# Norm weights applied to transposed blocks as they leave PSUM, and a shared rotary part copied by GpSimd

## The reference

```python
def _rms(x, g):
    y = xf * lax.rsqrt(jnp.mean(xf * xf, axis=-1, keepdims=True) + EPS)
    return (y * g).astype(x.dtype)
...
cq = (_rms(cq, w["c_cq_g"]) @ w["c_wuq"]).reshape(B, S, C_HEADS, C_QK)
cq = _rms(jnp.concatenate([cq[..., :C_NOPE], _rope(cq[..., C_NOPE:], pos)], axis=-1), w["c_qn_g"])
ckv = _rms(ckv, w["c_ckv_g"])
cpe = _rope(cpe[:, :, None, :], pos)[:, :, 0]
kv = (ckv @ w["c_wukv"]).reshape(B, nk, C_HEADS, C_NOPE + C_V)
ck = jnp.concatenate([kv[..., :C_NOPE], jnp.broadcast_to(cpe[:, :, None, :], (B, nk, C_HEADS, C_ROPE))], axis=-1)
ck = _rms(ck, w["c_kn_g"])
oc = _full_attend(cq[:, :, :, None], ck, kv[..., C_NOPE:], C_QK ** -0.5, q_start, prompt)

mq = _rms(mq.reshape(B, S, M_HEADS, HEAD_DIM), w["m_qn_g"])[:, :, :, None]
om = _attend(mq, mem_k, mem_v, None, HEAD_DIM ** -0.5)
```

## Time and profile before

| | us |
|---|---|
| median of 3 runs | 3257.39 (3252.74 to 3262.34) |
| the profiled execution | 3255.39 |
| its span, first to last instruction | 3253.6 |
| TensorE busy | 2920.4 (90%) |
| VectorE busy | 1807.6 (56%) |
| ScalarE busy | 1197.6 (37%) |
| GpSimd busy | 136.5 (4%) |
| mean granted TensorE clock | 0.936 |

### The profile page before, as it was taken

The page is one execution under the profiler, slowest core; times in us unless marked ns, Lnnn a source line. Parts: engine busy times, 40 slices in busy tenths (PEclk is TensorE's granted clock), DMA queues, the critical chain, the costliest instruction groups (busy, mean ns, idle before and its releaser), DMA issues. The chain is left out here.

```text
span 3253.6 us, 49067 instructions
## 1 busy us (share of the span) xinstructions
PE 2920.4 (90%) x19080; PEld 2750.4 (85%) x19080; DVE 1807.6 (56%) x2899; ACT 1197.6 (37%) x2503; POOL 136.5 (4%) x228
## 2 busy tenths in 40 slices
PE   5888879789899999999968888788789999999997
PEld 3787768579899999999957868667789999999997
DVE  5466765643555555554665586465436555545554
ACT  5556644652322222222246474456413222212222
POOL 0200012000000000000002000120000000000000
PEclk7996989799999999999979979898899999999999
DMA  4110001022111111111031100110411111111111
GB/s 177 32 57 30 23 29 39 8 86 82 52 46 46 41 50 40 46 45 48 20 124 47 48 22 21 40 29 11 150 28 51 47 45 46 43 50 46 40 46 61
DMA packets 182436, 162.11 MB, mean 50 GB/s; under 512 B 14648, under 2 KB 170040, under 8 KB 181688
## 3 DMA queue, kind: packets, MB, share of 16 engines
q1 hardware_dynamic: 182200, 158.81, 15.5%
HBM read 129.92 MB, written 29.06 MB: 49 GB/s over the span
## 5 line engine op out<-in xcount | busy, mean ns | idle before, releaser
L1752 PE MATMUL ps<-h_hi,w_hi 128*128 128x352 f32 x2496 | 550.5, 329 | 49.6 <-DVE w_lo L1863 23.1
L1752 PE MATMUL ps<-h_hi,w_lo 128*128 128x352 f32 x2496 | 544.6, 325 | 6.9 <-issue 6.9
L1752 PE MATMUL ps<-h_lo,w_hi 128*128 128x352 f32 x2496 | 543.1, 326 | 0.0
L1752 PEld LDWEIGHTS ps<-h_hi,w_hi 128*128 128x128 f32 x2496 | 430.3, 192 | 64.7 <-issue 42.2
L1752 PEld LDWEIGHTS ps<-h_hi,w_lo 128*128 128x128 f32 x2496 | 433.3, 190 | 0.0
L1752 PEld LDWEIGHTS ps<-h_lo,w_hi 128*128 128x128 f32 x2496 | 429.7, 190 | 0.0
L2203 ACT ACTIVATE cv<-up,cols 128x1058 f32<-128x1058 f32 x88 | 112.0, 1273 | 737.9 <-issue 697.8
L774 PE MATMUL ps<-w_hi,h_hi 128*128 128x256 f32 (+1 forms) x1152 | 334.5, 290 | 24.1 <-DVE w_lo L944 18.2
L775 PE MATMUL ps<-w_lo,h_hi 128*128 128x256 f32 (+1 forms) x1152 | 328.8, 285 | 0.0
L776 PE MATMUL ps<-w_hi,h_lo 128*128 128x256 f32 (+1 forms) x1152 | 326.6, 284 | 0.0
L2314 DVE TENSOR_TENSOR x_t<-ps,x_t 128x1056 f32<-128x1056 f32 x176 | 221.0, 1256 | 159.5 <-PE ps L1752 158.8
(11 more groups left out here) (211 smaller groups left out, 4275.7 us busy)
## 6 DMA issues: line engine op xcount, KB each, us to landing
stage<-in_f_win SPq DMA_DIRECT2D x88, 512.0 KB, 3.8
stage<-in_f_wout SPq DMA_DIRECT2D x44, 512.0 KB, 3.7
stage<-in_w_in SPq DMA_DIRECT2D x40, 256.0 KB, 4.4
x_spill<-x_t SPq DMA_DIRECT2D x2, 4224.0 KB, 14.3
x_t<-x_spill SPq DMA_DIRECT2D x2, 4224.0 KB
stage<-in_w_o SPq DMA_DIRECT2D x16, 512.0 KB, 4.5
w_raw<-in_w_in SPq DMA_DIRECT2D x24, 256.0 KB, 3.9
o_in<-o_spill SPq DMA_DIRECT2D x8, 528.0 KB, 7.1
```

The lines of the kernel that those rows point to most:

```text
L1752: last = pe.matmul(ps[:, s0 + b, 0:BAND], lh, rh_[:, b * BAND:(b + 1) * BAND], start=(first_k and n == 0), stop=(last_k and n == 2))
```

## The change

For three kinds of pieces (C's queries, C's keys, M's queries; `late_gain`) VectorE writes `res = zs * ri` at once and leaves the norm weight out. After the transposition the head's columns lie on partitions, so the weight is one number per partition: ScalarE multiplies by it in its copy of the high part, and VectorE in the low part, `lo = turned * gain - hi`. The weight tile has one column; it is loaded by DMAs with 4 bytes per partition, for M two of them, since a turned block holds two heads. ScalarE waits once per piece for it.

For C's keys (`shared`) GpSimd copies the rotary part into the four heads of `zs`. It waits for the result two steps back and for the producer of the part; ScalarE's squares wait for it. ScalarE's two remaining copies change places: `zs` first, then v.

```diff
 def first_gains(sp):
     for p in normed:
-        sp.dma_start(p.gain_t[:, :], p.gain.partition_broadcast(P)).then_inc(S.small_loaded, 16)
+        if p.late_gain:
+            for i in range(p.bw // p.hd):
+                sp.dma_start(p.gain_t[i * p.hd:(i + 1) * p.hd, :], p.gain.rearrange("(h o) -> h o", o=1)
+                             ).then_inc(S.small_loaded, 16)
+        else:
+            sp.dma_start(p.gain_t[:, :], p.gain.partition_broadcast(P)).then_inc(S.small_loaded, 16)
...
                     if p.after:
                         src, hi, _ = after_views(g)
-                        act.copy(hi, src).then_inc(S.tr_copied, 1)
+                        if p.late_gain:
+                            if s == 0:
+                                act.wait_ge(S.small_loaded, n_small)
+                                if n_scaled[id(p)]:
+                                    act.wait_ge(S.gain_scaled, n_scaled[id(p)])
+                            act.mul(hi, src, p.gain_t[0:p.bw, 0:1]).then_inc(S.tr_copied, 1)
+                        else:
+                            act.copy(hi, src).then_inc(S.tr_copied, 1)
...
+                if p.late_gain:
+                    dve.tensor_tensor(res[0:r, n % 2, 0:nt * n_el].rearrange("p (t h d) -> p t h d", t=nt, d=hd),
+                                      zv[:, :, 0:n_el].rearrange("p t (h d) -> p t h d", d=hd),
+                                      ri[0:r, 0:gh].rearrange("p (t h) -> p t h", t=nt).unsqueeze(3).broadcast_to([r, nt, H, hd]),
+                                      ALU.mult).then_inc(S.res_done, 1)
+                    return
...
-                dve.tensor_tensor(lo, src, hi.bitcast(F32), ALU.subtract).then_inc(S.tr_low, 1)
+                if p.late_gain:
+                    dve.scalar_tensor_tensor(lo, src, p.gain_t[0:p.bw, 0:1], hi.bitcast(F32), ALU.mult, ALU.subtract
+                                             ).then_inc(S.tr_low, 1)
...
+                if p.shared is not None:
+                    src, from_load, producer = p.shared(s)
+                    pool.wait_ge(S.res_done, n_i[g] - 1)
+                    if from_load:
+                        pool.wait_ge(S.data_loaded0, 16 * len(late_loads))
+                    else:
+                        q, qs = producer
+                        pool.wait_ge(S.res_done, n_i[at[id(q), qs]] + 1)
+                    zp = zs[0:r, n_i[g] % 2, 0:p.n_el].rearrange("p (h c) -> p h c", c=p.hd)
+                    pool.tensor_copy(zp[:, :, 64:96], src.unsqueeze(1).broadcast_to([r, 4, 32])).then_inc(S.pre_rotated, 1)
+                    continue
...
             def copies(t0, nt, r, bank, zs):
-                return [(v_big[0:r, v_tile(t0), :].rearrange("p (h c) -> p h c", c=64), b4[:, :, 64:128]),
-                        (z4[:, :, 64:96], cpe_of(t0, r).unsqueeze(1).broadcast_to([r, 4, 32])),
-                        (z4[:, :, 0:64], b4[:, :, 0:64])]
+                return [(z4[:, :, 0:64], b4[:, :, 0:64]),
+                        (v_big[0:r, v_tile(t0), :].rearrange("p (h c) -> p h c", c=64), b4[:, :, 64:128])]
```

More of the change, by code:

```diff
@@ L581, in pieces_stage @@
         for p in normed:
-            p.gain_t = (gains or w).take("gain", [P, p.hd])
+            p.gain_t = (gains or w).take("gain", [P, 1 if p.late_gain else p.hd])
         G = order or [(p, s) for p in pieces for s in range(len(p.steps))]
@@ L623, in pieces_stage @@
                     split_after[last_of[id(holders[i - 1])]] = p
-        n_small = 16 * len(normed)
+        n_small = 16 * sum(p.bw // p.hd if p.late_gain else 1 for p in normed)
         n_loads = 16 * len(loads)
+        n_scaled, scaled = {}, 0
+        for p in normed:
+            scaled += 1 if p.scale is not None else 0
+            n_scaled[id(p)] = scaled
         res_sem = (S.res_out0, S.res_out1)
@@ L1063, in gpsimd @@
                     norm.pool_low(pool)
-                steps = [g for g in range(NG) if G[g][0].rope_first]
+                steps = [g for g in range(NG) if G[g][0].rope_first or G[g][0].shared is not None]
+                turned_steps = 0
                 for i, g in enumerate(steps):
@@ L1706, in pieces_c, with keys @@
         lat = piece([(t, 1, P) for t in range(4)], raw=lambda s: lat_in[:, s, :], stack="raw", to=lambda t: (ckv_s, None, t * P))
[L1708 removed]
+        def keys(steps, latents, shared, v_tile, placed, to):
             def product(pe, t, r, out):
```

29 lines of the change are left out of this document (19 added, 10 removed).

## The result

| | before | after |
|---|---|---|
| median, same chip | 3257.63 (9 runs, 3249.49 to 3285.07) | 3240.98 (9 runs, 3230.68 to 3244.83) |
| ratio of the runs, 95% interval | | 0.993 (0.9904 to 0.9957) |
| profiled execution / span | 3255.39 / 3253.6 | 3230.68 / 3228.9 |
| mean granted clock in it | 0.936 | 0.940 |

The change gains 0.7% by the ratio of the runs (0.4 to 1.0%, 14 to 31 us), and 17 us between the two medians. The forecast was 12.4 us (3245.0, range 3239 to 3256; a ratio of 0.996). The sign was right, and the gain was larger than predicted. Medians in this document are over all runs of a kernel; ratios and intervals leave out slow ones, those over 1.5% above the fastest of the same kernel.

A forecast was written before the change was run, and what follows sets the result against it. VectorE was taken to pace the key tiles, TensorE nearly the queries. Per layer 2.95 (prompt keys) + 1.97 (cached keys) + 1.04 (C's queries) + 0.25 (M's queries) = 6.21, twice 12.4 us: 3245.0 us, range 3239 to 3256.

The forecast's parts named there:

- The bound and the loop: C's key tiles: VectorE paces at 2.33 us; afterwards the chain through ScalarE and VectorE paces at 2.01 us.
- Rival 1: Key tiles: VectorE and GpSimd block each other, loop 2.41 us, time 3254 on the median; chance 0.12.
- first failed step: C's queries: TensorE's wait for the latent's rotated part limits the gain to 0.26 four times, 1.04 us per layer.
- the first root's 0.42: First prompt key: its root comes 0.42 us earlier, as the last query tile ahead loses its gain step.
- Prompt to cached keys: Last prompt key's root to first cached key's: 0.49 us less per layer, from 0.29 and 0.20.
- M's queries: TensorE paces all but the last step; its last turn's wait for a result shrinks by 0.25 us per layer.
- Rival 2: Key tiles: ScalarE's longer copy and the GpSimd semaphore wait are not hidden, loop 2.15 us, time 3248; chance 0.23.
- The slack of 0.13 and 0.06: Key loop: the room in which ScalarE's longer copy and the extra wait on GpSimd's semaphore were to hide.
- second failed step: Clock at attention C's start: no term in the sum; layer 1 beginning like layer 2, 5 us better (3240), called inside the forecast.
- Rival 3: C's queries at half clock for 22 us per layer: 11 us lost in each, net 9.8 slower, 3267; chance 0.05.

The follow-up runs named there:

- keys_gain: Kernel before plus late gain for C's keys alone, ScalarE still copying the rotary part in the old order; 3266.62 us, ratio 1.002, key loop 2.20.
- keys_shared: Kernel before plus GpSimd's shared copy alone for C's keys, the gain still a VectorE step; 3253.89 us, ratio 0.9993, key loop 2.33.
- pool_eight: Changed kernel with GpSimd's shared copy made eight times in a row, each waiting for the one ahead; 3300.18 us in one execution, loop 3.15.
- only_queries: Kernel before plus late gain for C's queries alone, keys and M's queries as before; 3278.45 us, ratio 1.0092.
- psum_filler: Changed kernel plus a VectorE step as long as the gain step for each C query, one input in PSUM, result unused; 3281.73 us in one execution.
- queries_warm: Kernel with late gain on C's queries alone, plus five unused TensorE products a layer in waits around the last keys; 3236.51 us, ratio 0.9949.
- after_warm: Changed kernel plus five unused TensorE products a layer in waits around the last keys; 3228.32 us, ratio 0.9923.
- only_m: Kernel before plus late gain on M's queries alone, C as before; 3262.3 us, ratio 1.0018.
- delay kernels: Extra reciprocals at the second cached key: four in the kernel before (3297.81 us, ratio 1.0122), six in the changed kernel (3270.4 us, ratio 1.0038).
- second series: Both kernels run again unchanged, 12 runs each: before 3250.35 us, ratio 0.9985; changed 3237.01 us, ratio 0.9947.
- before_delay: Kernel before plus four more VectorE reciprocals of 0.2 us at each layer's second cached key tile; 3297.81 us, ratio 1.0122.

## Why the prediction was right and wrong

**The bound and the loop: right.** The key loop was forecast at 2.01 and measured at 2.00 to 2.01; each link of the chain is in the rows above. With it the first to last key rows of the table came within 0.07 us; for the cached keys that is in part luck, since the 9.56 us from which I took the 8.04 hold a late reciprocal of 0.35 that is no part of the loop and went away. keys_gain and keys_shared show that ScalarE's chain and VectorE's sum are both needed in the reading. Two sizes were off without effect: GpSimd's copy took 0.29 us where I took 0.46, and the scaled copy 0.67 where I took 0.69.

**Rival 1, the port: false in the keys, and missed in the queries.** pool_eight shows VectorE's reduction, low part and result beside a busy GpSimd at their own lengths. What gives way there is GpSimd, in the one copy beside the result step (0.70 us for 0.30), and in the changed kernel no copy stands there. But the same mechanism had a price before, where I did not look: GpSimd's rotation of the queries was held by two two-input steps, 0.35 us each. I had written that TensorE's wait for the latent's rotated part decides, and took 0.26 in four places, 1.04. This term is the first failed step: the row with queries and first root gave 2.06 instead of 1.46, and 2.09 in only_queries. Without the first root's 0.42 that is 1.65, inside my bounds of 0 and 2.2, of which 0.35 is the late reciprocal at the fifth query. The triples did not shorten by 0.26 each but by 0.96, 0.51, 0.29 (the late reciprocal in it) and -0.05; in each of them the way from one query to the next lost 0.36, and the way from the query to the latent 0.59, 0.22 and nothing, and gained 0.34 in the last. psum_filler leaves 1.1 of the 1.7, so GpSimd's freedom is the larger part. The Trainium skill (SBUF — State Buffer, section Who interferes with whom) has the rule for this: a VectorE instruction with at most one SBUF input, outside the two-port modes, does not contend with GpSimd. The runs agree on both sides (0.32 us beside the PSUM input, 0.64 beside two SBUF inputs). I had used the rule against the change and not for it.

**Prompt to cached keys: 0.98 instead of 0.49.** I counted this stretch at VectorE's and ScalarE's terms. It runs on TensorE at the half clock for most of its length; the turn of the last prompt key now comes before the fall, which stands 2.4 us behind that key's root and stood 1.6 behind it. Kept at the full clock, the stretch loses 1.40 us in queries_warm and 0.95 in after_warm.

**M's queries: right in place, lost in the time.** 0.25 per layer was forecast, from the last root to the table load 0.27 was measured (4.69 to 4.42 us). In every profile with M's late gain the last turn follows that root 0.27 us sooner than in those without. The whole of M's preparation differs by 2.5 us between repeats of one kernel, nearly all of it ahead of the third root, and only_m's time shows no gain.

**Rival 2 (loop 2.15): false.** The slack of 0.13 and 0.06 held.

**The clock: the second failed step, and the one that carried the time out of the range.** The sum charged it with nothing. Rival 3 looked only at queries slowed down, and put the better start of attention C at 5 us "inside my forecast". In fact that start is worth -4.0 in the profile (-3.4 in the repeats), it moves with the end of C's preparation, and the delay kernels show that such a shift is worth up to 27 us in one attention. How much of the gain is clock can be estimated. Over 105 runs of the kernel before (one of 4158.8 us left out), span against mean granted clock lies on a line of 2.8 us per 0.001, with a scatter of 2.9 us. At equal clock the changed kernel is 8.1 us (plus or minus 3.9) and, in its second series, 10.9 (plus or minus 2.3) below; its mean clock was 0.9399 and 0.9396 against 0.9376 (0.9379 in the second series alone), which is worth 5 to 6 us more. So of about 16 us, roughly 10 go with the work and 6 with the clock. This is coarse, for a low stretch costs less in a preparation than in an attention, and the account does not close: C's preparations alone are 14.1 us shorter in both pairs of profiles, some 4 more than the line leaves to the work. It is not the same 6 us in another kernel with the same edit.

What stays open: where those 4 us went, why the clock comes back sooner or later from the same busy TensorE (the rows have 91 matmuls in 22 us either way while it is low), and what the 2.5 us stalls and the late reciprocals wait for.

## What to carry to other kernels

Two engines that pass a tile back and forth have two bounds, each engine's sum and the chain through both; here each edit moved one of them, and alone one gave half of the gain and the other next to nothing. A per-row factor rides almost free in a PSUM copy that has to be made anyway (0.11 us on ScalarE, 0.07 on VectorE). And where TensorE's clock falls at the border of a long TensorE-bound stage, judge a small edit by the stretch that it touches, over root-to-root distances, and not by the median: shift the stage by pure delay first, to learn what a microsecond of shift is worth.

## What the runs showed of the hardware

- A delay under 2 us in a kernel of some 3255 us cost about 40 us (before_delay): the two attentions C grew by 50 us together in its profile, with 104 us more at the lower of the two clock levels (0.50), in stretches where TensorE is busy throughout.
- With 2.30 of 3.42 us of work on TensorE ahead of it the clock fell all the same (after_warm).
- Ten tiny instructions a layer took 14 to 19 us off the feed-forward parts: 14 stalls of up to 2.5 us, with no cause in the profile, became 2. That is as much as the whole change.
- A GpSimd step of 0.32 us takes 0.64 to 0.69 beside a VectorE step with two SBUF inputs, and 0.32 beside one of the same length with an input in PSUM. A GpSimd copy of 0.30 us takes 0.70 beside a two-input step. VectorE's result step beside it takes 0.56 to 0.62, as against 0.56.
- One VectorE reciprocal in the first cached key and one in the fifth query start 0.35 us late in both layers of every profile whose VectorE instructions ahead in the layer are those of the kernel before, and on time in all others.
